# The first two output products of an FFN chunk, each worked up to its last tile, then the last tile of each

## The reference, cut to what matters

```python
def swiglu(x, w_in, w_out):
    g, u = jnp.split(x @ w_in, 2, axis=-1)
    return (jax.nn.silu(g) * u) @ w_out
...
        yp = yp + mp
        ys = ys + ms
        yp = yp + swiglu(rmsnorm(yp, norm_ffn[i]), w_ffn_in[i], w_ffn_out[i])
        ys = ys + swiglu(rmsnorm(ys, norm_ffn[i]), w_ffn_in[i], w_ffn_out[i])
    y_prompt = rmsnorm(yp, norm_final)
    y_sample = rmsnorm(ys, norm_final)
```

## Time and profile before

| | |
|---|---|
| median of 3 timed runs | 3029.73 us |
| span of the profiled execution | 3031.1 us |
| TensorE busy | 2883.9 us (95%) |
| VectorE, ScalarE, GpSimd busy | 1258.7, 734.5, 1053.6 us |
| mean granted TensorE clock | 0.953 |

### The profile page before, as it was taken

One profiled execution on the slowest core, in us unless ns is written; L12 is line 12 of the kernel. 1 busy time (PEld: TensorE's weight loads), 2 busy tenths in 40 slices (PEclk: granted clock), 3 DMA queues, 4 the chain that ended last, 5 costly groups with the idle time before them and its releaser, 6 DMA issues.

```text
span 3031.1 us, 46736 instructions
## 1 busy us (share of the span) xinstructions
PE 2883.9 (95%) x18103; PEld 2669.3 (88%) x18103; DVE 1258.7 (42%) x1380; ACT 734.5 (24%) x991; POOL 1053.6 (35%) x450
## 2 busy tenths in 40 slices
PE   6899998999998899999999999999999999999997
PEld 4677776776775799999999999999999999999997
DVE  6867768667766332222122224344232222122224
ACT  3032233234233233111111113111233111111123
POOL 5334334424532243323223236222343223323234
PEclk8967989998897899999999999999999999999998
DMA  6535556556556511111111111111111111111112
GB/s 234 181 104 174 187 188 197 198 172 224 176 185 199 201 49 46 38 56 38 52 48 31 56 35 53 49 48 42 42 49 42 42 51 43 46 49 38 53 38 74
DMA packets 283765, 290.03 MB, mean 96 GB/s; under 512 B 11092, under 2 KB 244565, under 8 KB 283559
## 3 DMA queue, kind: packets, MB, share of 16 engines
q1 hardware_dynamic: 265730, 275.25, 28.8%
q10 hardware_dynamic: 17812, 12.63, 1.3%
q0 software_dynamic: 144, 1.05, 0.1%
HBM read 267.65 MB, written 21.28 MB: 95 GB/s over the span
## 4 chain that ended last, share of the span: by engine, by line
PE 78%; DVE 9%; issue 5%; ACT 3%; DMA 2%; POOL 2%; SPq 1%; DVEq 0%; ACTq 0%; POOLq 0%
PE PS L1004 66%; PE PS L1166 2%; PE PS L1177 2%; PE PS L1121 1%; DVE nmax L1649 1%; PE PS L1150 1%; PE PS L1179 1%; DVE s_raw L1556 1%; DVE pt_lo L1656 1%; DVE t L1809 1%; DMA vpage<-in_cache_v 1%; ACT pt_hi L825 1%; PE PS L1153 1%; PE PS L1152 1%; PE PS L1151 1%
## 5 line engine op out<-in xcount | busy, mean ns | idle before, releaser
L574 POOL TENSOR_TENSOR w_lo<-raw,w_hi 128x1024 fp32r<-128x1024 f32 (+1 forms) x217 | 521.2, 2402 | 1494.7 <-ACT w_hi L717 1494.7
L1004 PE MATMUL PS<-a_hi,w_hi 128*128 128x344 f32 x3288 | 702.4, 322 | 5.5 <-DVE xf L1436 4.5
L1004 PE MATMUL PS<-a_lo,w_hi 128*128 128x344 f32 x3288 | 698.1, 320 | 0.0
L1004 PE MATMUL PS<-a_hi,w_lo 128*128 128x344 f32 x3288 | 694.6, 320 | 0.0
L1004 PEld LDWEIGHTS PS<-a_hi,w_hi 128*128 128x128 f32 x3288 | 551.8, 188 | 6.4 <-DVE xf L1436 4.6
L1004 PEld LDWEIGHTS PS<-a_lo,w_hi 128*128 128x128 f32 x3288 | 556.8, 189 | 0.0
L717 ACT ACTIVATE w_hi<-raw 128x1024 fp32r<-128x1024 f32 (+1 forms) x217 | 229.4, 1057 | 1344.4 <-PE PS L1004 1312.8
L1004 PEld LDWEIGHTS PS<-a_hi,w_lo 128*128 128x128 f32 x3288 | 548.4, 188 | 0.0
L1415 DVE SCALAR_TENSOR_TENSOR t<-PS,rinv 128x1032 f32<-128x1032 f32 x112 | 138.1, 1233 | 876.2 <-PE PS L1004 874.3
L612 POOL TENSOR_TENSOR kpage<-kpage,q_bc 128x1024 f32<-128x1024 f32 x112 | 278.0, 2500 | 251.2 <-DMA kpage<-in_cache_k 250.9
L1004 PE MATMUL PS<-b_hi,w_hi 128*128 128x344 f32 x1440 | 309.3, 323 | 24.5 <-POOL b_lo L677 16.7
(11 more groups left out here) (224 smaller groups left out, 2639.7 us busy)
## 6 DMA issues: line engine op xcount, KB each, us to landing
kpage<-in_cache_k SPq DMA_DIRECT2D x128, 512.0 KB, 4.8
vpage<-in_cache_v SPq DMA_DIRECT2D x116, 512.0 KB, 4.1
raw<-in_w_ffn_in SPq DMA_DIRECT2D x88, 512.0 KB, 3.8
raw<-in_attn_w_qkvf SPq DMA_DIRECT2D x24, 512.0 KB, 5.8
wseg<-in_attn_w_qkvf SPq DMA_DIRECT2D x12, 1024.0 KB, 5.2
raw<-in_w_ffn_out SPq DMA_DIRECT2D x32, 384.0 KB, 3.4
raw<-in_conv_w_in SPq DMA_DIRECT2D x24, 512.0 KB, 3.8
raw<-in_w_ffn_out SPq DMA_DIRECT2D x32, 320.0 KB, 3.1
```

The lines of the kernel that those rows point to most:

```text
L574: gp.tensor_tensor(w_lo[s][:, 0:kts, 0:cols], raw[s][:, 0:kts, 0:cols], w_hi[s][:, 0:kts, 0:cols].bitcast(F32), ALU.subtract).then_inc(w_l ...
L1004: ins = pe.matmul(g[:, b, :], w[:, k, :], x[:, k, b * TB:(b + 1) * TB], start=k == 0 and n == 0, stop=k == kts - 1 and n == 2)
```

## The change

Where an output stage starts, the two first products were made one after the other, the first with a wait ahead of each of its tiles. Now the first is worked up to its last tile but one, then the second is opened and worked as far, then come the last tile of the first and the last tile of the second. In `final_product` the transposes of tile 0 stand behind both. The same instructions are issued; only TensorE's order changes.

```diff
             def out_product(kts):
 
-                product(0, b_hi, b_lo, kts, parts=bl)
-                product(1, b_hi, b_lo, kts)
+                open_product(0)
+                product_steps(0, b_hi, b_lo, range(kts - 1), kts, bl)
+                open_product(1)
+                product_steps(1, b_hi, b_lo, range(kts - 1), kts)
+                product_steps(0, b_hi, b_lo, [kts - 1], kts, bl)
+                product_steps(1, b_hi, b_lo, [kts - 1], kts)
                 with counted_loop(pe, 1, KT // 2, {wlo[0]: 1, wlo[1]: 1, evd[0]: 1, evd[1]: 1}) as i:
                     product(0, b_hi, b_lo, kts)
                     product(1, b_hi, b_lo, kts)
...
-                for m in range(KT):
-                    product(m % 2, b_hi, b_lo, kts, parts=bl if m == 0 else None)
-                    if m > 0:
-                        to_rows(m - 1)
+                open_product(0)
+                product_steps(0, b_hi, b_lo, range(kts - 1), kts, bl)
+                open_product(1)
+                product_steps(1, b_hi, b_lo, range(kts - 1), kts)
+                product_steps(0, b_hi, b_lo, [kts - 1], kts, bl)
+                product_steps(1, b_hi, b_lo, [kts - 1], kts)
+                to_rows(0)
+                for m in range(2, KT):
+                    product(m % 2, b_hi, b_lo, kts)
+                    to_rows(m - 1)
                 to_rows(KT - 1)
```

## The result

The changed kernel had a median of 3049.68 us in 8 runs, against 3030.26 us in 8 runs of the kernel before; the ratio is 1.0045, 95% interval [1.0025, 1.0066]. (It isn't the quotient of the two medians, which is 1.0064 and lies inside the interval.) Repeated in two later comparisons, the same kernel came out at 1.0018 [1.0003, 1.0032] and 1.0040 [1.0023, 1.0058]. So it is slower, by 0.2 to 0.45% by these ratios; I had forecast +7.3 us, 0.24%.

What follows compares the result with a forecast made beforehand. TensorE, busy 95% of the span, was taken as the bound, with holes at 8 FFN chunks. Order +5.8, old falls -3.05, new falls +4.6 give +7.3 us on 3029.7: 3037.0 us, range 3030.5 to 3046.5.

Steps and rivals of the forecast that it cites:

- The waits for b_lo: TensorE's idle before the first product's last tile, 1.55 us (6 tiles) or 2.94 (5), would go at all 8 FFN chunks.
- The release chain of 3.79 us: Slot 0's refill by ACT and POOL after the first product; one k (1.42 us) covers it, leaving nine 2.37 us holes.
- ACT's split of slot 0: ACT's writing of w_hi for the third product would come some 5.6 us later than before after a chunk.
- The order's sum of +5.8 us: All places without clock: 6-tile chunks +3.3, 5-tile -1.7, convolution +2.5, attention +1.7, final chunk 0.
- The convolution: Its output stage had no hole to lose, so the new hole is all loss: +2.5 us, once.
- The attention's +1.7 us: In the attention's output stage nothing is gained and the third product starts later, at 1034.76 instead of 1033.03.
- The final chunk at 0: Transposes for `yt` wait for DVE's scaling: a hole of 3.0 us replaces one of 2.94, no net change.
- The norm stages hide the square sum: POOL's 2.99 us square sum between its splits delays slot 1's w_lo, but stays hidden with 1.7 us of cover.
- the clock's term: TensorE clock falls to 1.2 GHz: two old ones go (-3.05 us), 3 of 10 new holes have one (+4.6 us).
- More than four cold stretches there: Sign of being wrong: TensorE's clock at 0.50 behind more than four new holes, where about 3 were forecast.
- The price of a fall: Each drop of TensorE's clock from 2.4 to 1.2 GHz behind a hole costs 1.5 us.
- its first rival: Clock falls at most new holes; nine falls give +16.5 us, 3046 us; chance of five or more 0.37.

Runs made afterwards that it cites:

- the third trace: The changed kernel run a third time with no edit; 2034.7 us from the attention's first output product to the end, with 5 clock falls.
- the first trace: First profiled execution of the changed kernel; span 3041.7 us, 2038.4 us from the attention's first output product to the end, clock falls at 8 of 10 new holes.
- 8-tile stages undone: Changed kernel with the attention's and convolution's output stages back in the old order, new order in FFN chunks alone; ratio 1.0030 [1.0013, 1.0048] against before.

## Why the prediction was right in kind, and where it was off

- The waits for b_lo go at all 8 chunks, and the second product opens free: right, none was left in any trace of the new order.
- The release chain of 3.79 us less one k: forecast rows of about 2.2 us nine times and 2.8 once; measured 2.23 to 2.25 nine times and 2.79 once. ACT's split of slot 0 was to come some 5.6 us later: it comes 15.8 us after TensorE turned to b (1256.68 - 1240.87) where it was 10.4 (1456.79 - 1446.42), so 5.4.
- The order's sum of +5.8 us: right in the FFNs. Less the falls, +0.5 us for FFN 0 was forecast (2 x 0.82 - 2 x 0.57) and 762.5 - (765.0 - 3.05) = 0.6 measured; for FFN 1 it is +1.1 forecast and 758.1 - 757.0 = 1.1. The convolution came to 376.2 - 373.6 = +2.6, from the third trace, which has no fall there, and the kernel with this stage undone; from the first trace less its fall it is 378.1 - 374.4 - 1.5 = +2.1; forecast 2.5. The two differ because the convolution's restart behind its wait of 4.99 us runs at 1.2 GHz for a time that varies: the clock over the first 5.0 us is 0.51 before, 0.59 in the first trace, 0.69 in the third and 0.70 in the kernel undone. The pair with like clocks gives the +2.6. The 5-tile chunks did gain and the 6-tile ones lost.
- The attention's +1.7 us: the stage grew by 4.3 us with a fall of 1.5, and 0.7 of it was a longer wait for DVE's b_lo (1.09 at 1015.55, against 0.35), so 2.0 or so. Whether the order has a part in that wait isn't shown; with the old order there (8-tile stages undone) it was 2.50 us once.
- The final chunk at 0: right, a hole of 2.79 for one of 2.79.
- The norm stages hide the square sum: right, no second wait at slot 1.
- The step that was mis-sized is the clock's term. I took 3 falls at 10 holes, 4.6 us; the traces had 8, 8 and 5, which is 12, 12 and 7.7. "More than four cold stretches there", one of the prediction's own signs of being wrong, was seen in all three. I had placed the new idle between the old ones of 1.39 us (four, no fall) and 2.79 (four, two falls) and gone below the latter. That step doesn't hold: the chance doesn't fall off evenly between the two lengths, and four holes are few to set a chance by, the more so as the falls aren't spread evenly over the places. Over all the kernels that have them, 25 of 36 holes of 2.2 us had a fall, against 8 of 12 for the old ones of 2.8 to 2.9.
- The price of a fall, 1.5 us, was right.

What came of it is +10.5 to +14.2 us in the stretch (+10.1 to +15.8 without the tails), where 7.3 was forecast; 3037.0 us was named. The ratio of 1.0045 puts the changed kernel at 3043.4 us on the base of 3029.7 that the forecast used, inside the range; its own median, 3049.7, lies above the range's end of 3046.5. The ratio's interval is +7.6 to +20 us, so the named difference of 7.3 lies just under it. The likeliest case of the text was two to four falls; what happened is its first rival, five or more, to which 0.37 was given. That the ratio still lands inside the range owes to the range having been drawn out to nine falls, and not to the falls that were chosen.

That the measured ratios run from 1.0018 to 1.0045 for one kernel isn't explained by the stretch, which differs by 4 us. The timed runs carry the attention's scatter (the two traces of before differ by 11.3 us ahead of the first output product), and I have no stages for them. That remains open.

## What to carry to other kernels

When work is interleaved to hide a late input, look at what the end of the first job releases: with one buffer in each slot, the time between the ends of two jobs is the cover of the next refill, and closing them up moves the wait instead of removing it. Here only as much of the second product as hides the late tile (two k) should go ahead, and the rest must stay behind to cover the 3.79 us of refill; that order gained 0.7 to 0.9% where the full interleave cost 0.2 to 0.45%. Count each hole in TensorE with the clock's price as well. Judge a change of this size by the stages in the trace rather than by totals that scatter by 10 us and more, and look in each stage for waits and falls that the change has no part in.

## What the runs showed of the hardware

A stand of 2.24 us between dense matmuls was enough for the granted clock to fall from 2.4 to 1.2 GHz in 25 of 36 cases; stands of 0.9 us (9 seen) and of 1.4 to 1.5 us (13 seen) never did it. Stands of 2.8 to 2.9 us did it no more often than those of 2.2 (10 of 16), nor did the one of 2.61 us ahead of the last transposes (6 of 11). The count leaves out the attention's waits for DVE's b_lo: one of 2.50 us had a fall, those of 1.98 and 2.16 us had none. A fall cost 1.5 us. TensorE working on unused data through the stand kept the clock up, and brought the stage to within 0.3 us of its time without falls.
